# A three-block model kernel on one core: activation buffers moved to another start address in SBUF

## The reference

```python
h = rmsnorm(x, norm_mix_g[layer])             # layer 0: RWKV-7 time mix, layer 1: conformer conv
x = x + out
x = x + memory_cross_attention(rmsnorm(x, norm_xattn_g[layer]), memn, w_q, w_kv, w_o)
u = causal_dwconv(rmsnorm(x, norm_ffn_g[layer]) @ w_in, dw)        # 1024 -> 5632
x = x + (silu(u[..., :D_FF]) * u[..., D_FF:]) @ w_out              # 2816 -> 1024
...
h = rmsnorm_2(x, norm_mix_g)                  # second block: h @ w_in (1024 -> 5160), GLA and FoX attention
x = x + y @ w_out
a, val = split(rmsnorm_2(x, norm_ffn_g) @ w_up)                    # 1024 -> 5632
return rmsnorm_2(x + (gelu(conv(a)) * val) @ w_down, norm_final_g)
```

## The kernel before

| buffer | start | modulo 64 | modulo 128 |
|---|---|---|---|
| wh, wl (weights) | 18432, 34816 | 0 | 0 |
| acth, actl | 67616, 84000 | 32 | 32 |
| common, tmp, sq, rstd | 103872, 105664, 109760, 113856 | 0 | 64 |
| zone (start of all that follows) | 115904 | 0 | 64 |
| hidh, hidl | 115904, 160960 | 0 | 64 |
| headh, headl, yh, yl, mixh, mixl, memh, meml, gmidh, gmidl | in zone | 0 | 64 |
| midh, midl (in the room of sq) | 109760, 111808 | 0 | 64 |

## Time and profile before

### The profile page before, as it was taken

How to read it: one execution, slowest core, us unless ns; L and a number is a source line. 1 busy time by engine, 2 the same in 40 slices (tenths; PEclk the granted TensorE clock), 3 DMA queues, 4 the chain that set the end, 5 groups by cost and what they waited for, 6 DMA issues and landing times.

```text
span 2819.8 us, 64649 instructions
## 1 busy us (share of the span) xinstructions
PE 2632.6 (93%) x26234; PEld 2470.4 (88%) x26234; DVE 1451.2 (51%) x2006; ACT 1158.7 (41%) x1666; POOL 947.3 (34%) x392
## 2 busy tenths in 40 slices
PE   4897899888999999999899999999999889999997
PEld 4885899687799999978697999999998758999997
DVE  6567544341267775289653677743143234655521
ACT  6542333435354443332543444334246532544432
POOL 1332000025234444433441344444443202444442
PEclk6998899989999999999899999999999999999999
DMA  2221000114122223322321222233222101222231
GB/s 106 75 86 57 4 5 5 65 54 156 60 69 92 100 90 105 104 98 74 106 83 38 90 89 97 98 105 117 85 91 72 42 5 53 98 89 90 100 103 65
DMA packets 61126, 219.92 MB, mean 78 GB/s; under 512 B 6688, under 2 KB 7072, under 8 KB 60320
## 3 DMA queue, kind: packets, MB, share of 16 engines
q1 hardware_dynamic: 57536, 206.43, 21.6%
q10 hardware_dynamic: 3424, 11.01, 1.0%
HBM read 213.22 MB, written 4.19 MB: 77 GB/s over the span
## 4 chain that ended last, share of the span: by engine, by line
PE 66%; issue 21%; DVE 8%; ACT 3%; POOL 3%; DVEq 0%; POOLq 0%; ACTq 0%
PE psum L504 59%; DVE psum L2229 5%; POOL wl L489 3%; PE psum L870 1%; PE psum L827 1%; PE psum L1045 1%; PE psum L1044 1%; DVE tmp L1837 0%; ACT wh L1135 0%; DVE fox_max L2422 0%; PE psum L1067 0%; PE psum L858 0%; DVE fox_p L2447 0%; PE psum L1047 0%; PE psum L547 0%
## 5 line engine op out<-in xcount | busy, mean ns | idle before, releaser
L489 POOL TENSOR_TENSOR wl<-raw,wh 128x1024 fp32r<-128x1024 f32 x388 | 947.1, 2446 | 1839.9 <-ACT wh L1135 1838.7
L504 PE MATMUL psum<-acth,wh 128*128 128x256 f32 x3808 | 769.8, 284 | 34.9 <-DVE actl L1794 18.1
L504 PE MATMUL psum<-actl,wh 128*128 128x256 f32 x3808 | 759.1, 281 | 0.0
L504 PE MATMUL psum<-acth,wl 128*128 128x256 f32 x3808 | 758.8, 281 | 0.0
L504 PEld LDWEIGHTS psum<-acth,wh 128*128 128x128 f32 x3808 | 587.8, 190 | 55.2 <-issue 30.8
L1135 ACT ACTIVATE wh<-raw 128x1024 fp32r<-128x1024 f32 x388 | 407.2, 1056 | 527.9 <-PE psum L504 527.4
L504 PEld LDWEIGHTS psum<-actl,wh 128*128 128x128 f32 x3808 | 587.3, 190 | 0.0
L504 PEld LDWEIGHTS psum<-acth,wl 128*128 128x128 f32 x3808 | 586.9, 190 | 0.0
L2159 DVE TENSOR_TENSOR cu<-psum,rstd 128x512 f32<-128x512 f32 x132 | 91.0, 690 | 235.1 <-PE psum L504 220.4
L504 PE MATMUL psum<-hidl,wh 128*128 128x256 f32 x1056 | 205.6, 276 | 0.0
L504 PE MATMUL psum<-hidh,wl 128*128 128x256 f32 x1056 | 205.6, 276 | 0.0
(11 more groups left out here) (409 smaller groups left out, 3985.0 us busy)
## 6 DMA issues: line engine op xcount, KB each, us to landing
raw<-in_weights SPq DMA_DIRECT2D x388, 512.0 KB, 3.4
xt<-in_x SPq DMA_DIRECT2D x4, 512.0 KB, 5.6
xt<-in_x ACTq DMA_DIRECT2D x1, 2048.0 KB, 9.3
out_x<-xt ACTq DMA_DIRECT2D x4, 512.0 KB, 2.9
mem<-in_mem ACTq DMA_DIRECT2D x1, 1024.0 KB, 11.1
memn<-memh ACTq DMA_DIRECT2D x1, 1024.0 KB, 3.9
memn<-meml ACTq DMA_DIRECT2D x1, 1024.0 KB, 6.8
memh<-memn ACTq DMA_DIRECT2D x1, 1024.0 KB, 7.0
```

Source lines behind the costliest of these rows:

```text
L489: pool.tensor_tensor(wl[:, s, :], raw[:, s, :], wh[:, s, :].bitcast(F32), ALU.subtract).then_inc(split_done, 1)
L504: ins = pe.matmul(out[:, n:n + HALF], w, m[:, n:n + HALF], start=first and n == 0, stop=last and n + HALF >= out.shape[1])
```

## The change

Two lines are added that move the cursor up to a multiple: to one of 128 ahead of `acth`, and to one of 64 ahead of the zone.

```diff
+        def aligned(to=128):
+
+            cursor[0] = (cursor[0] + to - 1) // to * to
+
...
         xt = place("xt", [P, KT, T + 1])
+        aligned()
         act_at = cursor[0]
         acth = place("acth", [P, KT, T], F32R)
         actl = place("actl", [P, KT, T], F32R)
...
         rstd = place("rstd", [P, T])
+        aligned(64)
         zone = cursor[0]
```

## The result

| | before | after |
|---|---|---|
| median | 2826.49 us | 2864.3 us (2861.29 to 2870.25, 4 runs) |
| the profiled execution | 2821.63 us | 2866.43 us |
| its span | 2819.8 us | 2864.6 us |
| mean granted clock | 0.965 | 0.968 |

The ratio is 1.013, with a 95% interval of 1.0103 to 1.0157: the change makes the kernel 1.3% slower, where 1% faster was forecast. The mean granted clock does not explain it: the slower execution was granted slightly more.

The account below looks back on a forecast made before the run. PE's `product` matmul spacing was taken to bound the kernel. A gain of 29.7 us on `acth`/`actl` less 0.3 for `midh`/`midl`, all else zero, gave 29.4 us off the median: 2797.1 us, range 2753 to 2832.

Parts of the forecast that it names:

- What bounds the kernel: Whole kernel: PE, busy 93% of the span, sets the end through the spacing of its `product` matmuls.
- Part 1: Stages reading `acth`/`actl`, moved to a multiple of 128: matmuls go from 116.7 to 113.3 ns, 29.7 us saved.
- nothing gained: Upper bound on the price of an `acth`/`actl` matmul at its new start: 116.7 ns, as before.
- Part 4: VectorE and ScalarE: `tmp` at 32 beyond 64 costs 0; the zone keeps its remainders, also 0.
- Part 2: Core buffers move to multiples of 128; `sq`, `rstd` and `common`, float32 operands, go the other way: zero for all.
- Part 3: `midh` and `midl` go to 32 beyond a multiple of 64: 96 float32r matmuls lose 0.3 us.
- No other engine becomes the bound: Up and down stages with faster PE: weights keep up, and DVE in up0 would be at 75%.
- Two levels: Stretches settle their spacing at restarts; one or two up stages, or all, at 117.8 ns: 2806 to 2836 us, chance 0.21.
- Full speed: `acth`/`actl` matmuls at a multiple of 128 run at or near 106.7 ns: 2738 to 2756 us, chance 0.17.
- Not the start: Distance to the weights counts, so `acth`/`actl` at 128 modulo 512 may stay at 116.7 ns: 2826 us, chance 0.16.
- Slower: Moving and stationary operands on the same multiple of 128 collide, `acth`/`actl` matmuls take 121.2 ns: 2866 us, chance 0.06.

## Why the prediction was wrong, point by point

- **What bounds the kernel: right.** PE's stream did, in spacing and not in waits. PE's busy time took the whole difference, and the arithmetic of the 3120-matmul pieces held in every kernel tried: 369.3, 364.7, 365.3, 353.6 us.
- **"What they share, and the `act` buffers lack, is the start at a multiple of 64": the reading that failed.** The fast buffers shared more, as the prediction itself says further down: 192 modulo 512, with the weights at 0. They all lie in one zone, so the trace of before held two starts, 32 and 192, and no third. Out of two points any rule could be read.
- **Part 1, the term that was mis-sized.** The new start was priced at 113.3, "nearest in kind"; it measured 118.67, above both bounds, since "nothing gained" was taken as the upper one. With 2.0 ns more in place of 3.33 less, the sum's 8784 matmuls give +17.6 us in place of -29.7. (The 8784 leave out the 144 of in2's last tiles, which the 29.7 hold; with them it is 8928.) The count of the up stages held: the piece of 353.64 us is 6.9 us shorter, 20.6 for all three, where the sum had 21.1. For the other stages it is not shown. The version with `act` at 192 gained 28 us by its ratio, where the sum was 29.4, but with in2's 480 and the second half of q0 at 117.8, and xo0 and xo1 slower than before, so that this agreement is in part luck, within an interval of 5 us.
- **Part 4, "The zone keeps its remainders: 0".** It keeps them modulo 128, not 256: from 192 to 64. That is 113.3 to 117.8 for the down stages, xo0, xo1 and out2, some 19 us by the spacings, 13.8 by the ratio of the zone alone. A term that I had put at nothing, because I had already settled what mattered. These are also the two levels that both starts know: the zone's cost is that its long stretches stand at the upper one at 64, where they stood at the lower one at 192. In the traces of the whole kernel at 256 columns the down stages were at 113.3 in fifteen of fifteen at distance 192, and at 117.8 in six of six at 64.
- **Part 2 and DVE: right as far as seen.** The 64x64 matmuls keep 218 ns, and DVE's groups of the earlier trace rows their means; no run moved `sq`, `rstd` and `tmp` alone. Part 3's start of 32 has the table's 116.7, as priced; 0.3 us can't be seen by itself.
- **No other engine becomes the bound: right**, tried at 353.6 us per piece: with `act` at 192, and with 512 columns.
- **The rivals.** *Two levels* exist and were named for the right reason, q1, but beside 37 us they are small: 2.3 us for up0 in the kernel moved by 128, 1824 x 4.45 ns = 8.1 us for the four stretches named in the version with `act` at 192. They also lie behind the zone's 19 us, a switch of whole stages that this rival did not foresee. *Full speed* falls: no start goes below 113.3, and the fit of two numbers to lines of 128 bytes did not hold for a third. The estimate of 109.2 ns from the Trainium skill ("TensorE: Matmul & The Clock Gate", Back-to-back issue gap), where the formula is given for an isolated matmul and not for a stream with weight loads, is not reached by any row of float32r matmuls here. *Not the start* had the mechanism, the distance to the weights, and put it at 0 instead of +37. *Slower* had the mechanism and the sign, with `act` at 121.2 alone; measured, 118.7 on `act` and 117.8 on the zone. Its 2866 is right, half of it for the right place. Against it I held that at half the clock the two reads "show no cost". That was no evidence. Timeline of after at half the granted clock, with the start that is slow at full:

```profile
48.24 0.63 PE L510 MATMUL psum<-acth,wh 128*128 128x256 f32 x2
48.66 0.63 PE L510 MATMUL psum<-actl,wh 128*128 128x256 f32 x2
```

Two matmuls in 0.42 us are 213 ns within the rows' hundredths, as in the earlier trace rows with the old start. A clock at which nothing shows says nothing of the other.

The chance for the two rivals that rest on the distance was 0.22 together. With only two starts in the trace, neither of them the new one, they deserved as much as the forecast, and the range should have reached as far above 2826 as below it.

## What to carry to other kernels

For a stream of float32r matmuls without idle time on PE, choose the buffers' starts relative to the weights' start, modulo 256, by measured spacing and not by how round the address is: 192 for 256 columns, 0 for 512, and every buffer behind a moved one has to be looked at again. One measuring kernel of under a millisecond gives the table, but it shows each start at the level that it has in that program, and in each version at 256 columns that had buffers at 192, some stretch on them ran at the slower one. When a trace shows only two values of a variable, put as much chance on a third value being worse as on its being better.

## What the hardware showed that I had not expected

- The spacing of float32r matmuls of 256 columns goes by the distance of moving start and weights' start modulo 256, from 113.3 ns (192) to 120.0 (0 and 96), and not in an order that alignment explains. Why the period is 256, and why 192 is best, stays open; separate distances for `wh` and `wl` were not tried.
- Most distances have two levels: 192 and 64 have 113.3 or 117.8, 32 has 116.7 or 117.8, 160 has 117.3 or 118.7, 128 has 118.7 or 120.0. A level is kept through a stretch of up to 2064 matmuls. Only one was seen for 0, 96 and 224.
- The best distance turns with the width: one matmul of 512 columns takes 226.9 ns at 0, where two of 256 take 240.
